# A hybrid decoder layer with a product-key expert mixer on one core: the up products in two passes over the tokens, and 160 instead of 128 tokens served by gathered rows

## What is computed

```python
qh = (xc @ w_query).reshape(chunk, PEER_HEADS, D_KEY)           # 8 heads
s1 = einsum('nhk,hmk->nhm', qh[..., :HALF_KEY], keys1)          # 128 scores
s2 = einsum('nhk,hmk->nhm', qh[..., HALF_KEY:], keys2)          # 128 scores
v1, i1 = top_k(s1, 16); v2, i2 = top_k(s2, 16)
cand = v1[..., :, None] + v2[..., None, :]                      # 256 sums
top, pos = top_k(cand, 16)                                      # idx = i1*128 + i2
g = softmax(top)
act = gelu(einsum('nd,nhkd->nhk', xc, expert_u[idx]))
out = einsum('nhk,nhkd->nd', g * act, expert_v[idx])
```

## Time and profile before

| | us |
|---|---|
| median of 3 runs | 2130.3 (2129.66 to 2133.02) |
| the profiled execution | 2130.92 |
| its span in the profile | 2129.3 |
| PE busy | 2009.3 (94%) |
| DVE busy | 1365.0 (64%) |
| POOL busy | 768.4 (36%) |
| ACT busy | 737.3 (35%) |

### The profile page before, as it was taken

The page is one execution under the profiler, slowest core; times in us unless marked ns, Lnnn a source line. Parts: engine busy times, 40 slices in busy tenths (PEclk is TensorE's granted clock), DMA queues, the critical chain, the costliest instruction groups (busy, mean ns, idle before and its releaser), DMA issues.

```text
span 2129.3 us, 39052 instructions
## 1 busy us (share of the span) xinstructions
PE 2009.3 (94%) x14822; PEld 1905.8 (90%) x14822; DVE 1365.0 (64%) x2428; ACT 737.3 (35%) x942; POOL 768.4 (36%) x493
## 2 busy tenths in 40 slices
PE   6988988898999999998899999999899999999999
PEld 6977763388999999998899999999899999999999
DVE  3669656403344487999788882200188897989885
ACT  4234663323222222332355553222223333333331
POOL 3332223222333333342221222343435545655550
PEclk9999999899999999999999999999999999999999
DMA  4435879631223333432344547343689999999992
GB/s 162 71 100 188 292 238 316 235 121 60 80 99 120 119 129 122 143 132 102 120 185 163 209 167 260 132 147 121 229 296 299 342 331 321 329 329 340 327 316 101
DMA packets 202170, 420.07 MB, mean 197 GB/s; under 512 B 28129, under 2 KB 137762, under 8 KB 189250
## 3 DMA queue, kind: packets, MB, share of 16 engines
q1 hardware_dynamic: 162866, 314.92, 43.2%
q0 software_dynamic: 32768, 100.75, 13.4%
q10 hardware_dynamic: 6416, 2.78, 1.0%
HBM read 350.46 MB, written 67.92 MB: 196 GB/s over the span
## 4 chain that ended last, share of the span: by engine, by line
PE 47%; issue 31%; DVE 9%; POOL 6%; ACT 3%; DMA 2%; DVEq 1%; SPq 0%; ACTq 0%; POOLq 0%
PE pair L1444 13%; PE pair L1446 13%; PE pair L1445 13%; POOL w_lo L576 6%; DVE conv L1010 2%; PE pair L1589 2%; DVE pair L1405 1%; DMA picked_a<-acts,at_unit 1%; DVE w_lo L1388 1%; PE pair L1601 1%; PE pair L1641 1%; PE pair L1554 1%; PE pair L1454 1%; PE pair L1576 1%; ACT page_kt L743 1%
## 5 line engine op out<-in xcount | busy, mean ns | idle before, releaser
L1444 PE MATMUL pair<-x_hi,w_hi 128*128 128x272 f32 x2560 | 757.4, 296 | 20.0 <-DVE x_lo L966 16.2
L1446 PE MATMUL pair<-x_hi,w_lo 128*128 128x272 f32 x2560 | 744.8, 291 | 0.0
L1445 PE MATMUL pair<-x_lo,w_hi 128*128 128x272 f32 x2560 | 742.9, 290 | 0.0
L576 POOL TENSOR_TENSOR w_lo<-w_raw,w_hi 128x2048 fp32r<-128x2048 f32 x64 | 301.5, 4711 | 621.4 <-ACT w_hi L836 621.4
L1444 PEld LDWEIGHTS pair<-x_hi,w_hi 128*128 128x128 f32 x2560 | 488.1, 191 | 23.2 <-issue 22.7
L1445 PEld LDWEIGHTS pair<-x_lo,w_hi 128*128 128x128 f32 x2560 | 487.7, 190 | 0.2
L1446 PEld LDWEIGHTS pair<-x_hi,w_lo 128*128 128x128 f32 x2560 | 486.5, 190 | 0.0
L1444 PE MATMUL pair<-a_hi,w_hi 128*128 128x416 f32 x1024 | 360.9, 352 | 12.7 <-DVE w_lo L1388 7.6
L1446 PE MATMUL pair<-a_hi,w_lo 128*128 128x416 f32 x1024 | 361.0, 353 | 0.0
L1445 PE MATMUL pair<-a_lo,w_hi 128*128 128x416 f32 x1024 | 358.5, 350 | 0.0
L854 ACT ACTIVATE act_out<-pair 128x544 f32<-128x544 f32 x128 | 81.3, 636 | 462.9 <-PE pair L1446 462.8
(11 more groups left out here) (202 smaller groups left out, 2610.0 us busy)
## 6 DMA issues: line engine op xcount, KB each, us to landing
w_raw<-in_u_t SPq DMA_DIRECT2D x64, 1024.0 KB, 5.8
acts<-act_out SPq DMA_DIRECT2D x64, 544.0 KB, 3.0
w_raw<-in_v_t SPq DMA_DIRECT2D x128, 256.0 KB
v_raw<-in_v_t SPq DMA_DIRECT2D x128, 256.0 KB
gates<-g_out SPq DMA_DIRECT2D x13, 2048.0 KB, 8.0
g_in<-gates SPq DMA_DIRECT2D x16, 1664.0 KB, 13.9
act<-acts SPq DMA_DIRECT2D x64, 416.0 KB, 6.1
v_ring<-in_cache_v SPq DMA_DIRECT2D x64, 256.0 KB, 3.9
```

The source lines that it names most:

```text
L576: pool.tensor_tensor(w_lo[:, slot, :], w_raw[:, slot, :], w_hi[:, slot, :].bitcast(F32), ALU.subtract).then_inc(u_lo_done, 1)
L1444: te.matmul(out, s_hi, m_hi, start=start, stop=False)
L1445: te.matmul(out, s_hi, m_lo, start=False, stop=False)
L1446: return te.matmul(out, s_lo, m_hi, start=False, stop=stop)
```

## The change

1. **Two passes.** U is read twice. Passes t = 0 to 63 make the up products of tokens 0 to 255, passes 64 to 127 those of tokens 256 to 543. A pass has 48 matmuls, of 256 or of 288 columns. Every pass loads its block of U again (three buffers now), and ACT and POOL split it again. POOL does the subtraction in two halves, one for each of the pass's two output blocks, and PE waits for a half at a time. From pass 90 on, the even passes are split by DVE in one piece.
2. **160 tokens by gathered rows.** NS = 160, ND = 384. For the 32 additional tokens, the 128 slots of a token are laid over four groups of 32 partitions, so that they take 32 more gathers (`MORE`): 160 gathers of rows and of activations in place of 128. A second `pick` computes their places, and SP moves their slots between partitions in four DMAs. Rows are gathered from pass 57 on, since the activations of the first 256 tokens are complete after pass 63: 14 rows are added between the one-hot matrices, 58 in passes 90 to 127, 88 beside the down chunks. The ring has six buffers. The sum of the first 128 slots stands in bank pair 3, that of the additional ones in bank pair 2; each is transposed and added in the end.
3. **Gates.** 12 chunks (96 groups) in place of 13, three groups in each of the passes 56 to 87.
4. **Down.** 384 columns in place of 416.
5. **Order.** 13 of the 24 score groups stand between the query chunks (7 before), 11 in passes 0 to 12. Exponentials after passes 18, 25, 32, 39, 46; transposes after 29, 36, 43, 50; gates and first activations are loaded at pass 91. The passes are written out where loops stood.

The core of the diff (`...` marks what is left out):

```diff
-ND = N - P
+FIRST = 256
+EXTRA = 32
+NS = P + EXTRA
+ND = N - NS
+SHARES = P // EXTRA
+MORE = SLOTS // SHARES
+ALL_ROWS = SLOTS + MORE
...
-RANK_STEPS = 32
-EXP_AFTER = (15, 18, 22, 25, 29)
-TURN_AFTER = (17, 20, 24, 27, 31)
+PASSES = 2 * STEPS
+EXP_AFTER = (18, 25, 32, 39, 46)
+TURN_AFTER = (22, 29, 36, 43, 50)
+GATES_FROM, GATES_PER_STEP = 56, 3
+ROWS_FROM, ROWS_FROM_CHUNK = 57, 5
+SPLIT_FROM = 90
+LOADS_AT = 91
+PREPARE_AT = (100, 104, 108, 112)
-RING = 5
+RING = 6
+GATE_ROWS = 2 * (NG - ROWS_FROM_CHUNK)
+LATE_ROWS = (ALL_ROWS - GATE_ROWS) * 2 // 5
...
+def tokens_of(t):
+    return slice(0, FIRST) if t < STEPS else slice(FIRST, N)
+def on_vector(t):
+    return t >= SPLIT_FROM and t % 2 == 0
+def gate_groups(t):
+    first = GATES_PER_STEP * (t - GATES_FROM)
+    return [g for g in range(first, first + GATES_PER_STEP) if 0 <= g < NG * GROUPS]
...
+            for t in range(PASSES):
+                if t + 3 < PASSES:
+                    wait_low_u(sp, t)
+                    load_u(t + 3)
+                if t:
+                    store_acts(t - 1)
...
-            with pool.Fori(0, STEPS // 2) as i:
-                for slot in range(2):
-                    split_u(2 * i + slot, slot)
+            def split_u(t):
+                pool.wait_ge(u_hi_done, t + 1)
+                for j in range(2):
+                    low, raw, high = (a.rearrange("p (k j i) -> p j k i", k=KD, j=2)[:, j]
+                                      for a in (w_lo[:, t % 2, :], u_raw[t % 3], w_hi[:, t % 2, :].bitcast(F32)))
+                    pool.tensor_tensor(low, raw, high, ALU.subtract).then_inc(u_lo_pool, 1)
...
+            for t in range(PASSES):
+                if not on_vector(t):
+                    split_u(t)
...
+                for k in range(late_rows(t), late_rows(t + 1)):
+                    fetch_ahead(k)
...
+            def high_u(t):
+                sc.wait_ge(u_loaded[t % 3], 16 * (t // 3 + 1))
+                wait(sc, up_done, 2 * t - 2)
+                sc.activation(w_hi[:, t % 2, :], u_raw[t % 3], ACT.Copy).then_inc(u_hi_done, 1)
...
+                    if c >= ROWS_FROM_CHUNK and w % 2:
+                        add_row(2 * (c - ROWS_FROM_CHUNK) + w // 2)
...
+            for t in range(SPLIT_FROM, PASSES):
+                if on_vector(t):
+                    split_u(t)
...
+                for k in range(late_rows(t), late_rows(t + 1)):
+                    add_row(k)
...
+            def up(t):
+                tokens = tokens_of(t)
+                groups = gate_groups(t)
+                slot = t % 2
                 for j in range(2):
+                    wait_low_u(te, t, j)
...
+                    wait(te, gelu_done, 2 * t + j - 3)
+                    made = bank(2 * slot + j)[:, 0:tokens.stop - tokens.start]
+                    for kd in range(KD):
+                        if kd == KD // 2:
+                            for g in groups[2 * j:2 * j + 1]:
+                                make_gates(g)
...
+                        last = product(made, stationary, (x_hi[:, kd, tokens], x_lo[:, kd, tokens]), kd == 0, kd == KD - 1)
+                    last.then_inc(up_done, 1)
```

506 lines of the change are left out of this document (268 added, 238 removed).

## The result

The changed kernel takes 2206.94 us (median of 4 runs, 2205.01 to 2209.92), the kernel before 2131.33 (2129.66 to 2133.02). The ratio is 1.0356, with a 95% interval of 1.0338 to 1.0374: slower by 76 us. The forecast was 2145, slower, with a range up to 2185. The direction was right; the time lies 22 us above the range.

A forecast was written before the change was run, and what follows sets the result against it. PE was taken to bound nearly everything, with a second engine close behind. Late passes ending at 1586 plus 557 us of down made a span of 2143; adding 1.6 gave 2145 us, range 2070 to 2185.

The forecast's parts named there:

- PE's rates: Up passes: 48 matmuls take 5.71 us at 256 columns and 6.39 us at 288, where nothing waits.
- the equal cost of the up products: Up products: 64 passes of 5.71 and 64 of 6.39 make 774 us, as before, so no gain.
- the start: Up steps begin at 612 instead of 607; passes 0 to 12 end at 695, the last ranking at 699.
- the collision of DVE and POOL: Doubled splits: POOL and DVE's two-SBUF-input operations exclude each other; each split holds DVE up for nothing or 4.2 us.
- Passes 13 to 55: Experts stage: 50 us a tile, chain ending at 963, gates from 992; PE loses 50 us.
- down: Down stage: 384-column matmuls save 43 us; less 3 for short stalls, plus 1, 601.9 becomes 557 us.
- The rival of unchanged down chunks: Down stage: a chunk stays at 9.07 us, paced by DMA, the 43 us missing: 2188; chance 0.03.
- gates: Passes 56 to 87: DVE and POOL in turn 320 us, added rows 10: 330, to 1322; PE waits 43.
- passes 88 to 127: Late passes: 256 us for PE plus 8 lost to POOL's splits and gathers, ending at 1586.
- The forecast's own range: Whole kernel: 2105 to 2165, for tiles of 47 or 53, gates of 315 or 340, gathers costing none or 14 us.
- The rival worse than forecast: Experts and late passes: tiles take 55 us (+25), DMA holds passes 90 to 127 (+6, +4): 2180; chance 0.17.
- gathers beside a split: Late passes: a gather beside DVE's split slows from 0.94 to 3.00 us; at 0.94 throughout, the forecast would be 2137.

The follow-up runs named there:

- Experiment 4: Changed kernel with GpSimd's subtraction for U's low parts covering one of eight column blocks in passes 0 to 87: 2092.68 us.
- experiment 8: Changed kernel with 8 instead of 58 rows of V in passes 90 to 127, the other 50 moved to the down chunks: 2200.62 us.
- Experiments 5 to 7: Changed kernel with all splits from pass 90 on VectorE, 2178.93 us; with activations gathered 16 rows ahead instead of 8, 2197.13 us; with both, 2165.17 us.
- experiment 7: Changed kernel with all late splits on VectorE and activations gathered 16 rows ahead: 2165.17 us.
- experiment 12: The spread version with the first loads for the down stage issued at separate passes instead of all at pass 107: 2109.73 us.
- the spread version: Changed kernel with late splits on VectorE, activations 16 rows ahead, gates 2 groups a pass over passes 56 to 103, 36 late rows: 2116.88 us.
- experiment 9: Changed kernel, late splits on VectorE, 8 late rows, VectorE's subtraction repeated in six passes to make TensorE wait; one execution, passes compared, no total time.

## Why the prediction was right in sign and wrong in size

**Right.** PE's rates (5.71 and 6.40 us a pass for 5.71 and 6.39), the equal cost of the up products, the start, and the collision of DVE and POOL as what the change meets. Passes 13 to 55 came out at 296.9 for 297: first expert operation at 698.05 (699), chain of five tiles ending at 956.0 (963), first gates after 990.2 (992). Experiment 4 shows that the 49 us lost there come with POOL's subtraction, and DVE waits only 5.6 us until its chain ends, so the chain is what sets the stage's length, as written. PE meets it at the exponentials and one turn: 14.8 of its 29.2 us of waits for POOL follow three waits of ACT for DVE's result. The low clock of this stage (0.95) wasn't foreseen; by this reading it costs nothing while DVE's chain is the limit.

**Right in sum by luck, half right in cause: down.** "64 x 48 x (0.1889 - 0.1749) = 43 us less" was given to width, with DVE's and DMA's room as a side remark. Alone, width gives 12 us. The sum came out because the change also takes 40 rows out of the stage, which the prediction counted for DVE and DMA but gave no part of the gain. The rival of unchanged down chunks, at 0.03, was nearer than I thought: with 138 rows there (experiment 8) the stage takes 594.6 us, about as long as with wide products and 88 rows (593.4). I should have seen it in the row used for the bound: DVE at 470 of 536 and DMA at 0.94 stand next to PE.

**Wrong: gates, +23.** The step "One after the other that is 10.0: 320 us ... So 330 us, to 1322, and PE waits 43". PE's waits measured 46.5: right. The sum of DVE's and POOL's work (320) was near too: DVE is busy 305 us. What failed is the step from these waits to the stage: it set what PE loses to its waits alone and put the low clock behind them at nothing. PE's 287 plus 46.5 is 333.5, 3.5 more than forecast; the other 19 us of the 23 have no wait to them. The clock was 0.94, the eleven passes named above have 1.3 to 2.3 us on top of their waits, and PE was busy 306.5 us, where experiment 4 shows 284.8 for the same matmuls; there the waits go, and the 19 us with them (288.6 for 287). The 3.5 are a second, smaller fault: I took DVE's and POOL's work one after the other as the pace, where DVE also waits for PE (42 us). I had seen "a slower clock after the first" in the kernel before and used it only to correct its own losses.

**Wrong: passes 88 to 127, +44.** The step "Together 13.5 us in 12.8: up to 14 us lost over 38 passes ... I take 8. The stage ends at 1586." That is a throughput of POOL alone, and POOL was indeed not full (240 of 308 us busy). The loss came from what stands behind what: activations asked for 8 rows ahead whose last gather had just been issued, with a split behind that wait on DVE; and splits on POOL behind gathers that wait for DVE's rows. Experiments 5 to 7 remove 22.7, 13.3 and, together, 34.3 us of the stage. Of what then is left, 9 us are the three passes after the first loads for the down stage (28.5 us for 19.2 in experiment 7; experiment 12 takes 9.5 out of the spread version), and most of the rest is the last pass, whose output stands behind a high part of V on ACT; in the changed kernel that is some 3 us. Of the 52 us lost in the changed kernel 31 are waits, 15 the low clock behind seven of them and 3 the last pass. So two terms of the step were wrong: waits of 31 us where it had 8, and a clock term that it hadn't.

The range also was too narrow at its upper end. The forecast's own range stops at 2165, while its terms there (a tile of 53, gates of 340, 14 us for gathers) add 15, 10 and 6 us to 2145 and make 2176; and no bound of it, nor of the rivals, had a clock term.

The rival worse than forecast (2180) had the place right, but its cause, DMA at 336 GB/s against 318 to 342, wrong. The stage moved 293 GB/s in the changed kernel, 333 once the orders were mended, and 353 in experiment 12, where passes without a wait still took 6.40 us. The Trainium skill, page SBUF — State Buffer, section SBUF: two separate sides, states about 358 GB/s between HBM and a core. Over a whole stage no run showed more than 353, and over 3.5 us one moved 396 (the second window behind the wait of 5.33 in experiment 9). By the page's figure the rival had no ground, and the runs agree.

On gathers beside a split, the trace after goes again against what the Trainium skill, page SBUF — State Buffer, section Who interferes with whom, infers, that a tensor_tensor leaves descriptor generation alone. Of the 120 gathers in the late passes the 26 that meet DVE's subtraction of U average 2.17 us, the other 94 average 0.95. By the page's inference all would be 0.94. In experiment 7, from 1400 to 1610 us, 42 that meet one average 1.74 and 57 others 0.94. The gathers here also read their row numbers from SBUF (`at_row`, `at_unit`); whether it is that read or the writing of descriptors that meets the subtraction, no run separates.

## What to carry to other kernels

When a change moves work between engines, a sum of rates per stage is a lower bound. Walk each in-order queue at the places where work was inserted: what does the instruction wait for, and which producer of the bounding engine stands behind it. Then add what the clock takes after a long wait of TensorE: in the gate and late stages of the changed kernel and in experiment 9 it was 1.3 to 2.8 us behind every wait of 2.5 us or more but one, and 0.2 to 0.3 behind waits of 1 to 2 us. And where two engines share a stage through two buffers, lower the demand per step (2 groups instead of 3) before looking for faster operations: that, with the rows shared out anew, gave 66 us here.

A stage has a second and a third limit close behind the first. Test a term such as narrower products by itself before crediting it: 12 us and 12 us alone were 46 together. And what one edit frees may be taken by the next limit: the late store of pass 91 cost nothing in the changed kernel and 8 to 11 us over passes 93 to 95 in experiments 5 to 7.
